# First token half of a decoder layer transposed straight from the loaded tiles, norm weights applied at the evacuation

## The chip, the cores and the metric

One NeuronCore of one Trainium2 chip runs the kernel. The metric is device time in microseconds; for the kernel before it is the median of three runs. All arithmetic is fp32. Every large product is done in three passes of fp32r matrix multiplications on a high and a low part of each operand (hi x lo, lo x hi, hi x hi), so each operand must be split in two before TensorE can use it.

## The reference, cut to what matters

```python
def rmsnorm(x, g):
    y = x * lax.rsqrt(jnp.mean(x * x, axis=-1, keepdims=True) + EPS)
    return y * g

n = rmsnorm(h, ln1_g)               # h: 1024 tokens x 1024 features
proj = n @ w_in                     # 1024 x 1536: pool | lru | gate columns
xc = causal_depthwise_conv(u_lru, conv_w, conv_b)
# y_pool from windowed means of u_pool; y_lru = rg_lru(xc, ...) * gelu(u_gate)
# rg_lru: r, i = sigmoid(xc @ w_a + b_a), sigmoid(xc @ w_i + b_i), then a linear scan over the tokens
h = h + concat(rmsnorm(y_pool), rmsnorm(y_lru)) @ w_out
h = h + (silu(n2 @ w_gate) * (n2 @ w_up)) @ w_down     # n2 = rmsnorm(h, ln2_g)
out = rmsnorm(h, lnf_g)
```

## The kernel before, in words

Tokens are in eight tiles of 128 (TT = 8), features in eight blocks of 128 (KT = 8). The input projection wants the normed input transposed, features on the partitions: `nT_hi` and `nT_lo`, 128 x 8 x 1024. It is made from units (c, i): column block c of `w_in` (twelve, of 128 columns; the lru columns first, then pool, then gate) by token half i (tiles 0 to 3, or 4 to 7). A unit is eight k-steps of three multiplications with 512 columns (`project`, L1622, through `three_pass`, L1598, lines 1602 to 1604). The order of the first units is (0,0), (1,0), (0,1), (1,1), then (2,0), (2,1) and so on (`UNITS`, L421).

Tile t of x is loaded whole by SP (L447 to L459), with the first two weight blocks between. Tiles 0 to 3 are only multiplied by the row of norm weights `g_row` (VectorE, `normalise`, L1124), since the root of the mean square of a token can be multiplied in later. Tiles 4 to 7 are multiplied by both (L1126), after ScalarE has squared and summed them (`x_squares`, L676, L669) and VectorE has made the reciprocal root (`variance`, `norm_rsqrt`). Each tile is transposed by TensorE in two lots of four 128 x 128 blocks, a bank each (`transposes`, L1609, L1619). ScalarE evacuates a bank as the high part (`nT_hi_part`, L662) and VectorE takes the difference as the low part (`nT_lo_part`, L1133). Weight blocks are split the same way: high part on ScalarE (`split_w`, L653), low part on GpSimd (L589).

The roots of tiles 0 to 3 are put on a diagonal (VectorE, L1167) and spread over the partitions by one product (`broadcast_roots`, L1698, L1700), which stands behind k-step 3 of unit (0,1). ScalarE copies it to `rb` (L703). `first_half` (VectorE, L1141) multiplies each unit of token half 0 by `rb` as it leaves its bank. On ScalarE the copy of `rb` stands in the queue ahead of the evacuations of units (0,0), (1,0) and (0,1), and of the split of weight block 2.

From the evacuated units of block j VectorE makes the convolution (`convolve`, L1199) and TensorE the gate products (`gates`, L1638, L1650): per call two fp32 multiplications, which show as four rows. `gates(j, 0)` waits for the convolution. Gates (0,0) stand behind unit (1,1) and ahead of unit (2,0); gates (0,1) behind unit (2,0). ScalarE takes the sigmoids (L751) and powers, VectorE the recurrence and its scan.

All queues are in order and written out by hand; semaphores tie them together. Then come the output projection, the FFN by Strassen-like products (L1730 to L1732) and the final norm; the change touches nothing of their order.

## Time and profile before

| | us |
|---|---|
| median of 3 runs | 925.41 |
| lowest, highest | 923.7, 925.44 |
| the profiled execution | 925.6 |
| its span, first to last instruction | 923.8 |
| TensorE busy in the span | 898.2 (97%) |
| VectorE, ScalarE, GpSimd busy | 617.0, 388.5, 317.3 |

Matrix multiplications are pipelined, so the rows of neighbours overlap: what one costs is the distance of its start from the next one's. Idle time is given with the instruction that ended it.

### The profile page before, as it was taken

To read this page: it belongs to the slowest core of one execution; us is meant where nothing else is said; L and a number is where in the kernel's file an instruction comes from. 1 tells how busy PE (TensorE), PEld (TensorE's weight loads), DVE (VectorE), ACT (ScalarE), POOL (GpSimd) and SP (SyncE) were. 2 spreads that over 40 slices of the span, in tenths; PEclk is the share of its full clock that TensorE was granted. 3 is DMA by queue.
4 is the path that set the end of the run, shared out by engine and by line. 5 is a ranking of instruction groups with operands and counts; after the bars stand their busy time and mean duration, and the time that the engine had idled before them with its cause. 6 is when DMAs were issued, how large, how long until landed. Compare 5 with 4: busy or idle time off the path is not lost.

```text
span 923.8 us, 10968 instructions
## 1 busy us (share of the span) xinstructions
PE 898.2 (97%) x3955; PEld 732.8 (79%) x3955; DVE 617.0 (67%) x822; ACT 388.5 (42%) x645; POOL 317.3 (34%) x227
## 2 busy tenths in 40 slices
PE   5989999999999999999999999999999999999996
PEld 4766777888888788888888888888888888888885
DVE  5568887546478865655665656656566986687766
ACT  5657623443365533323332323332334444444455
POOL 3023424364143655546555454545551000000000
PEclk9999999999999999999999999999999999999999
DMA  9011110203202132233322323224238943333324
GB/s 319 1 46 34 34 46 23 76 17 122 61 1 70 45 126 80 92 126 92 126 79 92 130 88 126 86 85 137 81 126 295 405 154 97 97 97 98 93 89 183
DMA packets 93790, 96.43 MB, mean 104 GB/s; under 512 B 5628, under 2 KB 63528, under 8 KB 93736
## 3 DMA queue, kind: packets, MB, share of 16 engines
q1 hardware_dynamic: 83224, 76.32, 24.3%
q10 hardware_dynamic: 10512, 19.40, 6.8%
q8 instruction: 32, 0.52, 0.2%
q14 instruction: 22, 0.18, 0.1%
HBM read 71.33 MB, written 24.38 MB: 104 GB/s over the span
## 4 chain that ended last, share of the span: by engine, by line
PE 91%; DVE 4%; issue 2%; ACT 1%; DMA 1%; POOL 0%; DVEq 0%; ACTq 0%
PE bank L1730 23%; PE bank L1731 23%; PE bank L1732 23%; PE bank L1602 7%; PE bank L1604 6%; PE bank L1603 6%; DVE xc L1199 2%; PE bank L1619 1%; PE bank L1650 1%; PE bank L1661 1%; DVE nT_lo L1133 1%; DMA g_row<-in_ln_g 1%; DVE xc L1124 0%; PE bank L1668 0%; ACT xc L734 0%
## 5 line engine op out<-in xcount | busy, mean ns | idle before, releaser
L624 POOL TENSOR_TENSOR r_lo<-wsum_S,r_hi 128x512 fp32r<-128x512 f32 x63 | 98.8, 1568 | 125.7 <-ACT r_hi L868 125.7
L624 POOL TENSOR_TENSOR r_lo<-gu_raw,r_hi 128x512 fp32r<-128x512 f32 x84 | 116.4, 1385 | 68.0 <-ACT r_hi L868 67.9
L1730 PE MATMUL bank<-T_hi,r_lo 128*128 128x512 f32 x336 | 130.9, 390 | 0.9 <-DVE u L1457 0.9
L1732 PE MATMUL bank<-T_hi,r_hi 128*128 128x512 f32 x336 | 130.7, 389 | 0.0
L1731 PE MATMUL bank<-T_lo,r_hi 128*128 128x512 f32 x336 | 130.7, 389 | 0.0
L1730 PE MATMUL bank<-d_hi,h_lo 128*128 128x512 f32 x308 | 119.8, 389 | 0.0
L1731 PE MATMUL bank<-d_lo,h_hi 128*128 128x512 f32 x308 | 119.8, 389 | 0.0
L1732 PE MATMUL bank<-d_hi,h_hi 128*128 128x512 f32 x308 | 119.8, 389 | 0.0
L868 ACT CAST r_hi<-gu_raw 128x512 fp32r<-128x512 f32 x84 | 52.3, 622 | 131.4 <-PE bank L1732 131.4
L1730 PE MATMUL bank<-nT_hi,r_lo 128*128 128x512 f32 x252 | 98.1, 389 | 0.0
L1731 PE MATMUL bank<-nT_lo,r_hi 128*128 128x512 f32 x252 | 98.0, 389 | 0.0
L1732 PE MATMUL bank<-nT_hi,r_hi 128*128 128x512 f32 x252 | 98.0, 389 | 0.0
L981 ACT CAST h_hi<-h_raw 128x512 fp32r<-128x512 f32 x76 | 47.2, 622 | 102.4 <-PE bank L1732 102.0
L1602 PE MATMUL bank<-nT_hi,w_lo 128*128 128x512 f32 x192 | 82.1, 428 | 2.4 <-DVE nT_lo L1133 2.4
L1435 DVE TENSOR_TENSOR h_lo<-h_raw,h_hi 128x512 fp32r<-128x512 f32 x76 | 52.4, 691 | 47.8 <-ACT h_hi L981 47.8
L1603 PE MATMUL bank<-nT_lo,w_hi 128*128 128x512 f32 x192 | 75.8, 395 | 0.0
L1604 PE MATMUL bank<-nT_hi,w_hi 128*128 128x512 f32 x192 | 75.7, 394 | 0.0
L1730 PEld LDWEIGHTS bank<-T_hi,r_lo 128*128 128x128 f32 x336 | 63.1, 188 | 14.7 <-POOL r_lo L624 1.3
L1731 PEld LDWEIGHTS bank<-T_lo,r_hi 128*128 128x128 f32 x336 | 63.1, 188 | 13.1
L1732 PEld LDWEIGHTS bank<-T_hi,r_hi 128*128 128x128 f32 x336 | 63.1, 188 | 13.0
L1732 PEld LDWEIGHTS bank<-d_hi,h_hi 128*128 128x128 f32 x308 | 57.8, 188 | 12.1
L1730 PEld LDWEIGHTS bank<-d_hi,h_lo 128*128 128x128 f32 x308 | 57.8, 188 | 12.0
(207 smaller groups left out, 1680.8 us busy)
## 6 DMA issues: line engine op xcount, KB each, us to landing
h_raw<-hid_ops ACTq DMA_DIRECT2D x72, 256.0 KB, 2.6
gu_raw<-in_w_ffn_gate SPq DMA_DIRECT2D x22, 512.0 KB, 3.7
gu_raw<-in_w_ffn_up SPq DMA_DIRECT2D x22, 512.0 KB, 4.8
hid_ops<-hid SPq DMA_DIRECT2D x44, 256.0 KB, 2.3
dn<-in_w_ffn_down SPq DMA_DIRECT2D x44, 256.0 KB, 10.8
hid_ops<-hsum_S SPq DMA_DIRECT2D x33, 256.0 KB, 2.6
w_raw<-in_w_in SPq DMA_DIRECT2D x12, 512.0 KB, 3.6
h<-in_x SPq DMA_DIRECT2D x8, 512.0 KB, 7.6
```

Source lines behind the costliest of these rows:

```text
L624: pool.tensor_tensor(lo_of(n)[:], a_block(f, name), f32(hi_of(n)[:]), ALU.subtract)\
L868: act.copy(hi_of(n)[:], a_block(f, name)).then_inc(r_hi_ok, 1)
L981: act.copy(h_hi[s % STEPS][:], h_source(s)[:]).then_inc(h_hi_ok, 1)
L1133: dve.tensor_tensor(nT_lo[dst], pt_of(n)[b][:].rearrange("p (k n) -> p k n", k=4), f32(nT_hi[dst]), ALU.subtract).then_inc(n_lo_ok, 1)
L1199: ins = dve.scalar_tensor_tensor(out=xc[j % 2][:], in0=ub[j % 2][:, off:off + S], scalar=v("conv_w", k * GT + j), in1=xc[j % 2][:], op0=AL ...
L1435: dve.tensor_tensor(h_lo[s % STEPS][:], h_source(s)[:], f32(h_hi[s % STEPS][:]), ALU.subtract)\
L1602: pe.matmul(bank, s_lo, m_hi, start=(k == 0), stop=False)
L1603: pe.matmul(bank, s_hi, m_lo, start=False, stop=False)
L1604: ins = pe.matmul(bank, s_hi, m_hi, start=False, stop=(k == n - 1))
L1730: pe.matmul(bank, s_lo, m_hi, start=(opens and j == 0), stop=False, skip_group_check=True)
L1731: pe.matmul(bank, s_hi, m_lo, start=False, stop=False, skip_group_check=True)
L1732: ins = pe.matmul(bank, s_hi, m_hi, start=False, stop=(closes and j == n - 1), skip_group_check=True)
```

## The change

Tiles 0 to 3 are loaded in left and right halves of 512 features. TensorE transposes each half as loaded, one bank of banks 2 to 5 for each tile, with no multiplication ahead of it. The norm weights are loaded as eight rows of 128, transposed on TensorE and copied to a column per feature block, `g_col`. The evacuation multiplies by them: four ScalarE operations of 128 columns with the column as scale in place of one cast of 512 (`first_hi`), and four VectorE operations in place of one (`first_lo`). The first two weight blocks are loaded and split in halves of four k-steps. Units (0,0) and (1,0) become four pieces of four k-steps (`project_first`): left halves of both units, then right halves; the right halves' transposes go between the k-steps of the first piece, those of tiles 4 and 5 into the third and fourth. The row of norm weights moves behind the fifth tile. The broadcast of the roots moves behind k-step 1 of unit (1,1). Gates (0,0) move behind unit (2,0). Two clears on GpSimd move behind the identity. In the FFN's down stage two semaphores of a pair of loads become one, with one threshold for both.

The diff, without the declarations of semaphores:

```diff
@@ -177,6 +177,8 @@
+g_rows = at("g_rows", 136.25, [KT, P])
+g_col = at("g_col", 140.25, [P, KT])
@@ -408,12 +419,19 @@
-FIRST_PT = ((6, 7), (0, 1), (2, 3), (4, 5))
 def pt_of(n):
-    return [psum[b] for b in (FIRST_PT[n] if n < 4 else (6, 7))]
+    return [psum[2 + n]] * 2 if n < 4 else [psum[6], psum[7]]
+def tile_count(n, b):
+    return 4 * b + n + 1 if n < 4 else 2 * n + b + 1
+def w_count(c):
+    return c + 3
 def sq_pos(n):
@@ -439,24 +457,26 @@
 def _(sp_q):
     def load_w_in(c):
-        if c >= 2:
-            sp_q.wait_ge(w_hi_ok, c - 1)
-            sp_q.wait_ge(w_lo_ok, c - 1)
+        sp_q.wait_ge(w_hi_ok, w_count(c - 2))
+        sp_q.wait_ge(w_lo_ok, w_count(c - 2))
...
-    def load_x(t):
+    def load_w_half(c, b, done_):
+        sp_q.dma_start(w_raw[:, c, KH * b:KH * (b + 1)], w_in_v[:, KH * b:KH * (b + 1), cols(COLS[c])])\
+            .then_inc(done_, 16)
+    for t in range(4):
+        sp_q.dma_start(h[:, t, 0:512], xf[cols(t), 0:512]).then_inc(x_left[t], 16)
+    for c in range(2):
+        load_w_half(c, 0, w_left[c])
+    for t in range(4):
+        sp_q.dma_start(h[:, t, 512:1024], xf[cols(t), 512:1024]).then_inc(x_in[t], 16)
+    for c in range(2):
+        load_w_half(c, 1, w_in_slot[c])
+    for t in range(4, TT):
+        if t == 5:
+            sp_q.dma_start(g_row[:], ln1_g.to_broadcast([P, D])).then_inc(grow_in, 16)
...
-    load_x(0)
-    load_x(1)
-    load_x(2)
-    load_w_in(0)
-    load_x(3)
-    load_x(4)
-    load_w_in(1)
-    load_x(5)
-    load_x(6)
-    load_x(7)
@@ -466,7 +486,7 @@
-    sp_q.wait_ge(zeroed, 2)
+    sp_q.wait_ge(zeroed, 3)
@@ -477,8 +497,8 @@
-            sp_q.wait_ge(w_hi_ok, NC_IN)
-            sp_q.wait_ge(w_lo_ok, NC_IN)
+            sp_q.wait_ge(w_hi_ok, w_count(NC_IN - 1))
+            sp_q.wait_ge(w_lo_ok, w_count(NC_IN - 1))
@@ -572,8 +592,6 @@
-    step(pool.memset(gate_w[0][:], 0.0))
-    step(pool.memset(gate_w[1][:], 0.0))
@@ -583,14 +601,22 @@
+    step(pool.memset(gate_w[0][:], 0.0))
+    step(pool.memset(gate_w[1][:], 0.0))
+    def split_w_half(c, b):
+        pool.wait_ge(w_hi_ok, 2 * b + c + 1)
+        k = slice(KH * b, KH * (b + 1))
+        pool.tensor_tensor(w_lo[c][:, k], w_raw[:, c, k], f32(w_hi[c][:, k]), ALU.subtract).then_inc(w_lo_ok, 1)
     def split_w(c):
-        pool.wait_ge(w_hi_ok, c + 1)
+        pool.wait_ge(w_hi_ok, w_count(c))
...
-    split_w(0)
-    split_w(1)
+    for b in range(2):
+        for c in range(2):
+            split_w_half(c, b)
@@ -652,6 +678,18 @@
+    def split_w_half(c, b):
+        act.wait_ge(w_in_slot[c] if b else w_left[c], 16)
+        k = slice(KH * b, KH * (b + 1))
+        act.copy(w_hi[c][:, k], w_raw[:, c, k]).then_inc(w_hi_ok, 1)
+    def first_hi(t, b):
+        act.wait_ge(xT_ok, tile_count(t, b))
+        for k in range(4):
+            ins = act.activation(nT_hi[:, 4 * b + k, cols(t)], pt_of(t)[b][:, cols(k)], ACT.Copy,
+                                 scale=g_col[:, 4 * b + k:4 * b + k + 1])
+        ins.then_inc(n_hi_ok, 1)
     def nT_hi_part(n):
@@ -674,18 +712,27 @@
     def x_squares(t):
+        if t < 4:
+            act.wait_ge(x_left[t], 16)
         act.wait_ge(x_in[t], 16)
         squares(t, t, sumA[:, PAD:])
-    act.dma_start(g_row[:], ln1_g.to_broadcast([P, D])).then_inc(grow_in, 16)
+    act.dma_start(g_rows[:], ln1_g.rearrange("o (k p) -> (o k) p", p=P)).then_inc(g_rows_in, 16)
+    act.wait_ge(consts, 2)
+    act.activation(early[:], ones[:], ACT.Sqrt)
+    act.wait_ge(gT_ok, 1)
+    act.copy(g_col[:], psum[1][:, 0:KT]).then_inc(g_col_ok, 1)
+    act.wait_ge(g_col_ok, 1)
+    for t in range(3):
+        first_hi(t, 0)
+    split_w_half(0, 0)
+    first_hi(3, 0)
+    split_w_half(1, 0)
+    for t in range(4):
+        first_hi(t, 1)
+    split_w_half(0, 1)
+    split_w_half(1, 1)
     act.wait_ge(consts, NCONST)
-    act.activation(early[:], ones[:], ACT.Sqrt)
-    nT_hi_part(0)
-    nT_hi_part(1)
-    split_w(0)
-    nT_hi_part(2)
-    nT_hi_part(3)
-    split_w(1)
     x_squares(4)
     x_squares(5)
     norm_sqrt(1, *BATCHES[0])
@@ -699,7 +746,7 @@
-    act.wait_ge(xs_ok, TT)
+    act.wait_ge(xs_ok, 4)
@@ -1112,19 +1159,15 @@
         rsqrt(var[:, lo:hi], sd[:, lo:hi], rstd[:, lo:hi], tmp[:, lo:hi], ready)
     def normalise(n, xs):
-        if n % TT >= 2:
+        if n % TT >= 2 and n not in (4, 5):
             dve.wait_ge(xT_ok, 2 * (n - 1))
-        if n == 0:
+        if n == 4:
             dve.wait_ge(grow_in, 16)
         if n == TT:
             dve.wait_ge(grow_in, 32)
             dve.wait_ge(proj_ok, 2 * NC_IN)
-        if n < 4:
-            dve.wait_ge(x_in[n], 16)
-            dve.tensor_tensor(xs[n % 2][:], h[:, n, :], g_row[:], ALU.mult).then_inc(xs_ok, 1)
-        else:
-            dve.scalar_tensor_tensor(out=xs[n % 2][:], in0=h[:, n % TT, :], scalar=rstd[:, n:n + 1],
-                                     in1=g_row[:], op0=ALU.mult, op1=ALU.mult).then_inc(xs_ok, 1)
+        dve.scalar_tensor_tensor(out=xs[n % 2][:], in0=h[:, n % TT, :], scalar=rstd[:, n:n + 1],
+                                 in1=g_row[:], op0=ALU.mult, op1=ALU.mult).then_inc(xs_ok, 1)
     def nT_lo_part(n):
         for b in range(2):
@@ -1140,15 +1183,20 @@
+    def first_lo(t, b):
+        dve.wait_ge(n_hi_ok, tile_count(t, b))
+        for k in range(4):
+            dst = (slice(None), 4 * b + k, cols(t))
+            ins = dve.scalar_tensor_tensor(out=nT_lo[dst], in0=pt_of(t)[b][:, cols(k)],
+                                           scalar=g_col[:, 4 * b + k:4 * b + k + 1], in1=f32(nT_hi[dst]),
+                                           op0=ALU.mult, op1=ALU.subtract)
+        ins.then_inc(n_lo_ok, 1)
+    dve.wait_ge(g_col_ok, 1)
+    for b in range(2):
+        for t in range(4):
+            first_lo(t, b)
...
-    normalise(0, xc)
-    normalise(1, xc)
-    normalise(2, xc)
-    nT_lo_part(0)
-    normalise(3, xc)
-    nT_lo_part(1)
-    nT_lo_part(2)
-    nT_lo_part(3)
@@ -1492,8 +1540,7 @@
     def down_sum(name, k):
...
-            dve.wait_ge(dn_in["22", k], 16)
-            dve.wait_ge(dn_in["12", k], 16)
+            dve.wait_ge(dn_in["22", k], 32)
@@ -1606,13 +1653,23 @@
+    def first_transposes(t, b):
+        if b == 0:
+            pe.wait_ge(x_left[t], 16)
+        else:
+            pe.wait_ge(x_in[t], 16)
+            pe.wait_ge(n_lo_ok, tile_count(t, 0))
+        for k in range(4):
+            ins = pe.transpose(pt_of(t)[b][:, cols(k)], h[:, t, cols(4 * b + k)], ident[:])
+        ins.then_inc(xT_ok, 1)
     def transposes(n, xs):
-        pe.wait_ge(xs_ok, n + 1)
+        pe.wait_ge(xs_ok, n - 3)
...
-            if 4 <= n <= TT:
-                pe.wait_ge(n_lo_ok, b + 1 if n == 4 else 2 * (n - 1) + b + 1)
+            if 5 <= n <= TT:
+                pe.wait_ge(n_lo_ok, 2 * (n - 1) + b + 1)
@@ -1622,7 +1679,7 @@
     def project(c, i, between=()):
...
-            pe.wait_ge(w_lo_ok, c + 1)
+            pe.wait_ge(w_lo_ok, w_count(c))
@@ -1686,24 +1743,44 @@
         three_pass(pj[n % 4][:], [(hi[:, k], lo[:, k], wo_hi[q][:, k], wo_low(q, k))
                                   for k in range(GT)]).then_inc(op_ok, 1)
-    pe.wait_ge(consts, NCONST)
+    def project_first(c, b, between=()):
+        pe.wait_ge(w_lo_ok, 2 * b + c + 1)
+        pe.wait_ge(n_lo_ok, 4 * (b + 1))
+        for k in range(KH * b, KH * (b + 1)):
+            n_hi, n_lo = nT_hi[:, k, half(0)], nT_lo[:, k, half(0)]
+            pe.matmul(pj[c][:], w_hi[c][:, k], n_lo, start=(k == 0), stop=False)
+            pe.matmul(pj[c][:], w_lo[c][:, k], n_hi, start=False, stop=False)
+            ins = pe.matmul(pj[c][:], w_hi[c][:, k], n_hi, start=False, stop=(k == KT - 1))
+            if k in between:
+                between[k]()
+        if b == 1:
+            ins.then_inc(proj_ok, 1)
+    pe.wait_ge(consts, 1)
+    pe.wait_ge(g_rows_in, 16)
+    pe.transpose(psum[1][:, 0:KT], g_rows[:], ident[0:KT, 0:KT]).then_inc(gT_ok, 1)
     for t in range(4):
-        transposes(t, xc)
-    project(0, 0, {6: lambda: transposes(4, xc)})
+        first_transposes(t, 0)
+    project_first(0, 0, {k: (lambda t=k: first_transposes(t, 1)) for k in range(4)})
+    pe.wait_ge(g_col_ok, 1)
+    project_first(1, 0)
+    project_first(0, 1, {5: lambda: transposes(4, xc)})
+    project_first(1, 1, {4: lambda: transposes(5, xc)})
     pe.wait_ge(rows_in, 16 * 8)
     pe.transpose(pg[0][:, 0:NROWS], vrows[0:NROWS, :], ident[0:NROWS, 0:NROWS]).then_inc(vT_ok, 1)
-    transposes(5, xc)
-    project(1, 0, {1: lambda: transposes(6, xc), 4: lambda: transposes(7, xc)})
+    transposes(6, xc)
+    transposes(7, xc)
     def broadcast_roots():
         pe.wait_ge(diag_ok, 4)
         pe.matmul(pg[1][:], ones_sq[:], diag[:], start=True, stop=True).then_inc(bcast_ok, 1)
-    project(0, 1, {3: broadcast_roots})
-    project(1, 1)
-    gates(0, 0)
+    project(0, 1)
+    project(1, 1, {1: broadcast_roots})
     for c in range(2, NC_IN):
         project(c, 0)
+        if c == 2:
+            gates(0, 0)
         if 0 <= c - 2 < GT:
             gates(c - 2, 1)
         if 0 <= c - POOL0 - 2 < GT:
```

## Rows read from the trace of the kernel before

**Rows 1.** The head of the page, and the chain that ended last, by engine

```profile
span 923.8 us, 10968 instructions
...
PE 91%; DVE 4%; issue 2%; ACT 1%; DMA 1%; POOL 0%; DVEq 0%; ACTq 0%
```

**Rows 2.** Busy time by stretch; after each engine's busy time the granted clock, DMA share, GB/s

```profile
17.00:20.50 3.50, 3.50 (x9) 2.73 (x10) 1.63 (x7) 3.08 (x8) 1.55 (x1) 0.51 1.15 321
27.50:31.00 3.50, 2.82 (x17) 2.10 (x16) 2.48 (x3) 2.44 (x6) 0.00 (x0) 1.00 0.00 0
51.00:54.50 3.50, 3.50 (x8) 1.83 (x7) 3.16 (x11) 1.65 (x3) 1.49 (x1) 0.52 0.21 56
120.00:200.00 80.00, 79.47 (x347) 63.41 (x346) 56.17 (x52) 27.75 (x38) 37.58 (x18) 1.00 0.15 47
```

**Rows 3.** TensorE in order of time: start, duration, line, operation, count

```profile
7.63 5.35 PE L1619 MATMUL bank<-ident,xc 128*128 128x128 f32 x24 [7.63 <-DVE xc L1124]
...
16.90 0.64 PE L1602 MATMUL bank<-nT_hi,w_lo 128*128 128x512 f32 x1 [2.41 <-DVE nT_lo L1133]
17.33 0.63 PE L1603 MATMUL bank<-nT_lo,w_hi 128*128 128x512 f32 x1
...
23.37 1.04 PE L1619 MATMUL bank<-ident,xc 128*128 128x128 f32 x8
...
26.55 1.16 PE L1619 MATMUL bank<-ident,xc 128*128 128x128 f32 x8 [1.26 <-DVE nT_lo L1133]
...
32.86 1.03 PE L1619 MATMUL bank<-ident,xc 128*128 128x128 f32 x8
...
38.51 1.02 PE L1700 MATMUL bank<-diag,ones_sq 128*128 128x512 f32 x2
...
39.61 0.40 PE L1603 MATMUL bank<-nT_lo,w_hi 128*128 128x512 f32 x1
...
47.35 0.39 PE L1604 MATMUL bank<-nT_hi,w_hi 128*128 128x512 f32 x1
50.34 2.99 PE L1650 MATMUL bank<-xc,gate_w 128*128 128x512 f32 x4 [2.60 <-DVE xc L1199]
...
60.61 0.79 PE L1602 MATMUL bank<-nT_hi,w_lo 128*128 128x512 f32 x1
```

**Rows 4.** DMA in the first 6 us

```profile
DMA packets 339, 1.26 MB, mean 210 GB/s; under 512 B 32, under 2 KB 32, under 8 KB 339
```

**Rows 5.** ScalarE in order of time

```profile
12.74 1.08 ACT L662 CAST nT_hi<-bank 128x512 fp32r<-128x512 f32 x2
...
15.05 1.06 ACT L653 CAST w_hi<-w_raw 128x1024 fp32r<-128x1024 f32 x1
15.99 1.07 ACT L669 ACTIVATE sumA<-h 128x1024 f32<-128x1024 f32 x1
...
39.57 0.59 ACT L703 COPY rb<-bank 128x512 f32<-128x512 f32 x1 [3.43 <-PE bank L1700]
...
72.04 0.69 ACT L751 ACTIVATE rg<-bank,vec 128x512 f32<-128x512 f32 x1
72.62 0.68 ACT L751 ACTIVATE ig<-bank,vec 128x512 f32<-128x512 f32 x1
```

**Rows 6.** VectorE in order of time

```profile
13.08 3.67 DVE L1133 TENSOR_TENSOR nT_lo<-bank,nT_hi 128x512 fp32r<-128x512 f32 x6
...
19.86 2.48 DVE L1126 SCALAR_TENSOR_TENSOR xc<-h,rstd,g_row 128x1024 f32<-128x1024 f32 x2
...
34.12 1.29 DVE L1133 TENSOR_TENSOR nT_lo<-bank,nT_hi 128x512 fp32r<-128x512 f32 x2 [1.76 <-ACT nT_hi L662]
...
37.11 0.88 DVE L1167 TENSOR_SCALAR diag<-ident,rstd 128x128 f32<-128x128 f32 x4
```

**Rows 7.** GpSimd in order of time, the third weight block

```profile
45.25 2.63 POOL L589 TENSOR_TENSOR w_lo<-w_raw,w_hi 128x1024 fp32r<-128x1024 f32 x1 [26.70 <-ACT w_hi L653]
```

More of the change, by code:

```diff
@@ L188, in sem @@
             return ctx.enter_context(nc.semaphore(name))
+        x_left = [sem(f"x_left{t}") for t in range(4)]
         x_in = [sem(f"x_in{t}") for t in range(TT)]
+        w_left = [sem(f"w_left{c}") for c in range(2)]
+        g_rows_in = sem("g_rows_in")
         rows_in, grow_in, small_in = sem("rows_in"), sem("grow_in"), sem("small_in")
@@ L198, in hymba_pool_rglru_block @@
         h_raw_in = [sem(f"h_raw_in{s}") for s in range(STEPS)]
-        dn_in = {bk: sem(f"dn_in{bk[0]}_{bk[1]}") for bk in DN_ORDER}
+        dn_in = {bk: sem(f"dn_in{bk[0]}_{bk[1]}") for bk in DN_ORDER if bk[0] != "12"}
+        for k in range(NP):
+            dn_in["12", k] = dn_in["22", k]
         stored = sem("stored")
@@ L215, in hymba_pool_rglru_block @@
         vec_ok = sem("vec_ok")
+        g_col_ok = sem("g_col_ok")
         u_ok = sem("u_ok")
@@ L266, in hymba_pool_rglru_block @@
         vT_ok = sem("vT_ok")
+        gT_ok = sem("gT_ok")
         bcast_ok = sem("bcast_ok")
@@ L986, in split_dn @@
                 if pr in ("M1", "M2", "M3"):
-                    act.wait_ge(dn_in[D_BLOCK[pr], k], 16)
+                    act.wait_ge(dn_in[D_BLOCK[pr], k], 32 if pr == "M3" else 16)
                 else:
```

## The prediction

> **What bounds the kernel now.** I read first the head of the page and its chain of waits [rows 1]: 91% of the chain that ended last is TensorE, in a span of 923.8 us; the profiled execution took 925.6 us, so 1.8 lie around the span, and the median of the runs shown is 925.41, 0.2 below it. The sum below is made against 925.6 and shifted by that 0.2. Next the stretches [rows 2]: between 120 and 200 us TensorE is busy 79.47 of 80 us. So a microsecond that TensorE gains or loses before about 120 us reaches the end, unless VectorE's chain of the mixer takes it back. Third, TensorE in order of time [rows 3]. The start holds four losses: nothing until 7.63; a stop from about 14.5 to 16.90; the half clock after it; and 2.60 us before the first gates at 50.34, again followed by a half clock. The granted clock is 0.51 and 0.52 in 17 to 20.5 and 51 to 54.5 and 1.00 in 27.5 to 31, where TensorE was busy 2.82 of 3.5 us [rows 2]: the 1.2 and the 2.4 GHz level. A product instruction takes 0.43 us at the lower one (16.90 to 17.33) and 0.228 at the higher: 34 steps from 39.61 to 47.35 [rows 3].
>
> **Step 1, the start.** Before, the 512 KB of the norm's row go first and the first multiplication waits for them. They leave the front; instead 4 KB of weights are loaded, transposed and copied to a column. By 6.0 us 1.26 MB had moved [rows 4]. The four left halves are 1.05 MB, so they are in by about 5.4 plus some 0.5 us, the first near 3.5 to 4. Identity and ones move ahead of two 0.5 us clears on GpSimd, hidden. I take ScalarE's first evacuation at 4.3.
>
> An evacuation of one bank was one cast of a 0.49 us pitch (two in 1.08) [rows 5]. It becomes four of 128 columns with a scale from the column. No such row exists. Bounds: a quarter of the cast each, 0.12, so 0.5 us a bank; from above the 0.69 of a sigmoid less 384 columns, 0.35 each, 1.4 a bank. The nearest row is the pair of sigmoids with one column operand, 72.04 to 72.62: 0.58 pitch at 512 columns; less the 384 columns that a piece lacks, at 0.88 ns each (a 1024-column cast has a pitch of 0.94, 15.05 to 15.99, so 512 columns cost 0.45), 0.24. That is 1.0 us a bank, and I take 1.05 with the last one's drain. VectorE: six banks in 3.67 us were 0.6 each; the four 128-column operations of the diagonal took 0.88 [rows 6], so 0.85 a bank (0.6 to 1.1).
> The Trainium skill, ScalarE: Activation LUTs, section What ACT_TABLE_LOAD costs, says that each pointer operand adds some 93 ns, whatever the columns; the rows agree (0.49 against 0.58). By its formula a bank would be 1.17 us and the sum some 0.3 us larger.
>
> So ScalarE: three banks 4.3 to 7.5, half a weight split 0.5, fourth bank to 9.1; VectorE to 10.2; GpSimd's half of a low part (half of the 2.63 of [rows 7]) is done by 9.6. The first product starts near 10.2, not 16.90: 6.7 us early.
>
> **Step 2, the right halves.** From 10.2 TensorE alternates three products and four transposes, at the lower clock at first: to 16.4 us. ScalarE's last bank follows to 17.6, two half splits to 18.6. Only then do the squares of x4 start: 18.6, before 15.99 [rows 5], **2.6 us later**. The lead of 6.7 is TensorE's only.
>
> **Step 3, the second token half.** Squares at 15.99 gave the first scaled tile at 19.86 + 1.24 = 21.1 [rows 6], 5.1 us later; it then waited for TensorE until 23.37 [rows 3]. After: 18.6 + 5.1 = 23.7, transposes at 23.9. TensorE has only two more k-steps by then, which themselves wait for GpSimd's low part of the right weight half (19.6), and from 21.0 it idles 2.9 us: the lead is gone. The chain of scale, transposes, cast and low part follows from 23.9. The transposes of tile 5 wait for tile 4's low part after the scaling of tile 6: about 28.6, before 26.55; tile 7's had waited 32.86 for products and come at 33.8. The second low part of tile 7 ends 3.0 later, near 36.8 (before 34.12 + 1.29 = 35.4). Products on the second half need all of them: 36.8 against 38.51 less twelve products of 0.228 = 35.8: **+1.0**.
>
> **Step 4, the clock.** Between 30 and 36.8 nothing but the transposes of tiles 6 and 7 is left for TensorE. I take the lower clock at 36.8: nine products at 0.43, not 0.228, **+1.8**. From below it is 0.
>
> **Step 5, the broadcast of the roots.** It stood behind four of eight k-steps of the first second-half unit; now it stands behind that unit and two k-steps: 30 products, not 12, 18 x 0.228 = **+4.1**. It comes at 38.51 + 1.0 + 1.8 + 4.1 = 45.4. The diagonal is ready at about 39 (before 37.11 + 0.88), so nothing asked for the delay.
>
> **Step 6, who is queued behind it.** ScalarE waits in order for the broadcast (39.57, after an idle 3.43) [rows 5]; behind it stand three evacuations and the split of the third weight block, whose low part on GpSimd ended at 45.25 + 2.63 = 47.88 [rows 7]. By +6.9 this is 54.8. Before, the gates at 50.34 hid it. Now the product behind which the gates are put needs it at once; TensorE is free at 36.8 + 48 x 0.228 + 1.8 + 0.9 (broadcast) = 50.4 and **idles 4.4 us**: one wait replaces the 2.6 of before. Then 24 products at first at the lower clock, 5.5 + 1.8 = 7.3, to 62.1. The gates' column input, ready at 50.3 before, is ready at 57.2: covered. Eight gate instructions at 0.43 (1.88 for four with the drain) are 3.4: the next unit starts at 65.5; before at 60.9 (60.61 in [rows 3] with the overlap of its start). **Sum +4.6**; VectorE's recurrence of head pair 0 moves by about the same, as it starts from those gates, so nothing gives it back.
>
> Other edits. More, smaller loads: SP issues all well ahead of their use; nothing. The norm's row lands near 14, first used past 22: nothing. The three small waits changed and the merged semaphores of the down stage: both blocks load in turn, and ScalarE's step there runs ahead: nothing, up to 0.3 us if it is late.
>
> Sum: 925.6 + 4.5 = 930.1 by the profiled execution, 929.9 by the median.
>
> **The rivals.** (a) The clock holds at 36.8, as it did with 2.82 of 3.5 us busy. Then the terms lose 1.8: +2.7 in the gates, and up to another 1.7 less where later TensorE stalls absorb it: 926.6 to 928.1, say 927.5. Against it: TensorE has under 2 us of work in the last 6. Chance 0.15.
> (b) Faster. The evacuation pieces cost near their lower bound, 0.5 us a bank, and the loads land early; ScalarE then has the squares at 14.6, 1.4 before their old time, and the second-half products start near 32.8, 3.0 early, with a warm clock. The broadcast is then only 1.1 late, and with 2.6 us saved before the gates the whole is 2 to 3 us shorter: 922.9. It decides from squares at about 15 us and the higher clock together. For it: TensorE's start is 6.7 us early for sure. Against it: the sigmoid row. Chance 0.14.
> (c) The two cancel, squares near 16 to 17: within 1.8 us, 925.4. Chance 0.13.
> (d) Pieces at their upper bounds, or low parts on VectorE held while GpSimd works: squares at 22, +7: 932.5. Chance 0.10.
> (e) The forecast, 0.48.
>
> **Numbers.** Measurements tell 0.2% (1.85 us) from no change. Faster: (b), 0.14. Same: (c) and a part 0.04 of (a), 0.17. Slower: the rest, 0.69. The range, from 924.0, which leaves out most of (b), to 932.0, which leaves out most of (d), holds about 0.8.
>
> **What would show it.** In the changed profile: first product near 10.2; squares of x4 near 18.6; TensorE idle some 3 us before tile 4's transposes; second-half products near 36.8 at a granted clock near 0.5; broadcast near 45; TensorE waiting 4 us on GpSimd's low part of the third block near 55. Wrong, if the squares start by 15 or the broadcast by 41: then the later stop is small and the gates' move wins.

## The result and the profile after

The changed kernel took 930.8 us (median of 4 runs, 930.02 to 931.72) against 924.74 us for the kernel before on the same chip: a ratio of 1.0063, 95% interval 1.0051 to 1.0075. It is slower, by 5.8 us by that ratio and 6.1 by the two medians. The forecast was 929.9 us, in a range of 924.0 to 932.0. The prediction started from a median of 925.41 for the kernel before, so what it forecast was a loss of 4.5 us. The profile is of the slowest of the four executions (931.72).

The head of the page, and the chain that ended last, by engine. They answer to [rows 1]:

```profile
span 929.9 us, 11022 instructions
...
PE 91%; ACT 3%; DVE 3%; issue 2%; POOL 1%; DMA 0%; ACTq 0%; DVEq 0%
```

The span is 6.1 us longer. The share of the chain says as little as it did before; the difference lies in the first 70 us. This is TensorE in order of time there, from its timeline (start, duration, line, operation, count, and the idle time before with what ended it). In the changed file L1663 is a transpose of a loaded half, L1751 a product of `project_first`, L1676 a transpose of tiles 4 to 7, L1649 a product of `project`, L1776 the broadcast, L1707 a gate product. The rows answer to [rows 3]:

```profile
7.59 1.11 PE L1663 MATMUL bank<-ident,h 128*128 128x128 f32 x4 [0.64 <-DMA h<-in_x]
11.29 0.77 PE L1751 MATMUL bank<-nT_lo,w_hi 128*128 128x512 f32 x1 [2.58 <-DVE nT_lo L1190]
...
26.02 1.09 PE L1676 MATMUL bank<-ident,xc 128*128 128x128 f32 x8 [2.61 <-DVE xc L1169]
...
30.60 1.10 PE L1676 MATMUL bank<-ident,xc 128*128 128x128 f32 x8
...
33.90 1.09 PE L1676 MATMUL bank<-ident,xc 128*128 128x128 f32 x8
36.05 1.16 PE L1676 MATMUL bank<-ident,xc 128*128 128x128 f32 x8 [1.06 <-DVE nT_lo L1176]
38.67 0.50 PE L1649 MATMUL bank<-nT_hi,w_lo 128*128 128x512 f32 x1 [1.47 <-DVE nT_lo L1176]
...
45.63 1.02 PE L1776 MATMUL bank<-diag,ones_sq 128*128 128x512 f32 x2
...
55.00 0.80 PE L1649 MATMUL bank<-nT_hi,w_lo 128*128 128x512 f32 x1 [4.22 <-POOL w_lo L614]
...
63.47 3.78 PE L1707 MATMUL bank<-xc,gate_w 128*128 128x512 f32 x8
66.69 0.79 PE L1649 MATMUL bank<-nT_hi,w_lo 128*128 128x512 f32 x1
```

Two rows of the kernel before that are compared here (the first product on the second token half, and the third stop for a convolution), and the third stop in the changed kernel:

```profile
35.79 0.39 PE L1602 MATMUL bank<-nT_hi,w_lo 128*128 128x512 f32 x1
98.12 1.98 PE L1650 MATMUL bank<-xc,gate_w 128*128 128x512 f32 x4 [1.20 <-DVE xc L1199]
```

```profile
104.21 1.98 PE L1707 MATMUL bank<-xc,gate_w 128*128 128x512 f32 x4 [1.18 <-DVE xc L1247]
```

What is to be seen. The first product starts at 11.29, not 16.90: 5.6 us early. Tile 4's transposes start at 26.02, not 23.37: the lead has become a lag of 2.7. The products on the second token half start at 38.67 against 35.8 before: +2.9. The broadcast comes 6.96 us behind them, before 2.7 us: +7.1 in all. Unit (2,0) starts at 55.00 after a stop of 4.22 us for a low part from GpSimd, and unit (2,1) starts at 66.69, before at 60.61: +6.1, which is the whole difference in span. Later the third stop for a convolution stands at 104.21 against 98.12, still +6.1, so nothing is given back.

ScalarE in order of time. L689 is the scaled evacuation, L684 the split of half a weight block, L707 the squares, L750 the copy of the roots, L679 the split of the third weight block. The rows answer to [rows 5]:

```profile
8.85 1.14 ACT L689 ACTIVATE nT_hi<-bank,g_col 128x128 fp32r<-128x128 f32 x4
9.86 0.63 ACT L684 CAST w_hi<-w_raw 128x512 fp32r<-128x512 f32 x1
13.80 1.14 ACT L689 ACTIVATE nT_hi<-bank,g_col 128x128 fp32r<-128x128 f32 x4 [3.31 <-PE bank L1663]
15.93 1.14 ACT L689 ACTIVATE nT_hi<-bank,g_col 128x128 fp32r<-128x128 f32 x4 [0.99 <-PE bank L1663]
17.55 2.27 ACT L689 ACTIVATE nT_hi<-bank,g_col 128x128 fp32r<-128x128 f32 x8 [0.48 <-PE bank L1663]
...
20.73 1.08 ACT L707 ACTIVATE sumA<-h 128x1024 f32<-128x1024 f32 x1
...
46.69 0.59 ACT L750 COPY rb<-bank 128x512 f32<-128x512 f32 x1 [7.28 <-PE bank L1776]
...
51.25 1.03 ACT L679 CAST w_hi<-w_raw 128x1024 fp32r<-128x1024 f32 x1
```

The squares of x4 start at 20.73, before at 15.99. ScalarE is idle 3.31, 0.99 and 0.48 us between the banks, since the evacuations in front of the squares wait for TensorE. In this trace the second-half products start 17.94 us behind these squares. Further on the copy of the roots follows an idle 7.28 us, and the split of the third block stands behind it until 51.25 (before 44.13).

GpSimd and VectorE around the third block, before in [rows 7]: L614 is the low part of a block, here two back to back, and L1247 the first convolution (from the two engines' timelines):

```profile
52.36 5.90 POOL L614 TENSOR_TENSOR w_lo<-w_raw,w_hi 128x1024 fp32r<-128x1024 f32 x2 [29.41 <-ACT w_hi L679]
```

```profile
51.46 7.88 DVE L1247 SCALAR_TENSOR_TENSOR xc<-ub,vec,xc 128x1024 f32<-128x1024 f32 x3 [2.80 <-ACT xc L781]
```

The first of the two low parts releases TensorE at 55.00. The convolution takes 7.88 us. In the kernel before it took 5.94, with one low part inside it:

```profile
44.34 5.94 DVE L1199 SCALAR_TENSOR_TENSOR xc<-ub,vec,xc 128x1024 f32<-128x1024 f32 x3 [2.80 <-ACT xc L734]
```

The granted clock by stretch (columns: stretch, its length, busy time of PE, PEld, DVE, ACT and POOL, granted clock, DMA share, GB/s), as [rows 2]:

```profile
11.20:16.80 5.60, 5.51 (x17) 4.53 (x18) 1.12 (x4) 2.01 (x8) 0.63 (x1) 1.00 1.06 412
26.00:30.40 4.40, 4.38 (x17) 3.46 (x17) 3.96 (x10) 2.21 (x5) 0.00 (x0) 0.62 0.21 63
31.00:38.60 7.60, 5.15 (x32) 3.83 (x30) 5.04 (x7) 6.14 (x11) 0.00 (x0) 1.00 0.01 2
38.60:50.60 12.00, 11.93 (x50) 9.31 (x50) 3.26 (x14) 4.45 (x11) 0.00 (x0) 1.00 0.00 0
55.00:61.30 6.30, 6.30 (x15) 4.95 (x16) 5.92 (x13) 0.68 (x1) 3.26 (x1) 0.51 0.56 166
```

After the 4.2 us stop TensorE runs at the lower level (0.51) for some 6.2 us, while the products from 38.6 ran at 1.00. The 1.00 of the first row can't be right: the products step by 0.43 us there (11.85, 12.28, 12.71), as they do from 55.00.

### The profile page after: what moved, and what is told of

It is laid out like the page before. It is cut to its first block, busy times and chain, and to the rows that moved or that the text cites. A ratio compares the mean times of both kernels' runs of the same rounds, so it can differ in the third digit from the quotient of the medians.

```text
span 929.9 us, 11022 instructions
## 1 busy us (share of the span) xinstructions
PE 902.5 (97%) x3956; PEld 734.4 (79%) x3956; DVE 615.3 (66%) x842; ACT 393.0 (42%) x672; POOL 318.2 (34%) x229
## 4 chain that ended last, share of the span: by engine, by line
PE 91%; ACT 3%; DVE 3%; issue 2%; POOL 1%; DMA 0%; ACTq 0%; DVEq 0%
PE bank L1807 23%; PE bank L1808 23%; PE bank L1809 23%; PE bank L1649 6%; PE bank L1651 6%; PE bank L1650 6%; PE bank L1676 1%; DVE xc L1247 1%; PE bank L1707 1%; PE bank L1718 1%; ACT nT_hi L689 1%; PE bank L1751 0%; PE bank L1725 0%; PE bank L1663 0%; ACT sumA L707 0%
## 5 line engine op out<-in xcount | busy, mean ns | idle before, releaser
L1649 PE MATMUL bank<-nT_hi,w_lo 128*128 128x512 f32 x176 | 75.1, 427 | 5.7 <-POOL w_lo L614 4.2
L1807 PEld LDWEIGHTS bank<-T_hi,r_lo 128*128 128x128 f32 x336 | 63.1, 188 | 14.7 <-POOL r_lo L650 1.3
L1650 PE MATMUL bank<-nT_lo,w_hi 128*128 128x512 f32 x176 | 69.7, 396 | 0.0
L1651 PE MATMUL bank<-nT_hi,w_hi 128*128 128x512 f32 x176 | 69.7, 396 | 0.0
## 6 DMA issues: line engine op xcount, KB each, us to landing
dn<-in_w_ffn_down SPq DMA_DIRECT2D x44, 256.0 KB, 10.2
```

The costliest lines, as they stand in the source:

```text
L1649: pe.matmul(bank, s_lo, m_hi, start=(k == 0), stop=False)
L1650: pe.matmul(bank, s_hi, m_lo, start=False, stop=False)
L1651: ins = pe.matmul(bank, s_hi, m_hi, start=False, stop=(k == n - 1))
L1807: pe.matmul(bank, s_lo, m_hi, start=(opens and j == 0), stop=False, skip_group_check=True)
```

## The experiments

All ratios are to the kernel before, run on the same chip in the same rounds. The median of the kernel before was 925.24 in the first group (e1 to e4), 925.57 in the second (e5 to e8) and 925.35 in the third.

The changed kernel was not run again in these rounds. Differences to it are differences of medians; by the ratios they come out up to 0.7 us otherwise (e1 6.0 instead of 5.7, e2 3.4 instead of 3.7, e7 4.3 instead of 3.6). The order of the kernels doesn't hang on that.

The start also varies from execution to execution. In e1, e2, e3 and e7 the code is the changed kernel's up to the second half, and in their traces the squares of x4 start at 19.96, 20.50, 19.84 and 20.32 and the second-half products at 37.91, 38.44, 37.78 and 38.25, against 20.73 and 38.67 in the changed kernel's trace.

**e1: the broadcast back.** In the changed kernel:

```diff
-            project(0, 1)
-            project(1, 1, {1: broadcast_roots})
+            project(0, 1, {3: broadcast_roots})
+            project(1, 1)
```

> The changed kernel with one thing undone: the broadcast of the roots stands again behind k-step 3 of unit (0,1). Theory A (the delay of the broadcast is passed on by ScalarE's queue to the third weight block, which unit (2,0) needs at once): the second-half products still start near 38.7 us, the broadcast comes at 41.4 instead of 45.63, the low part of the third block ends near 50.8 instead of 55.0, when TensorE comes free at 50.6; the wait of 4.2 us and the half clock behind it (2.9 us) both go, and the time falls by 6 to 7 us, to about 924. Theory B (the start decides: ScalarE's and VectorE's pieces make the second token half late): the broadcast only matters by its own 4.1 us or less, and the time stays near 927 to 930.

Measured: 925.11 us, ratio 0.9998 (0.9989 to 1.0007): 5.7 us below the changed kernel. TensorE's timeline:

```profile
37.91 0.50 PE L1649 MATMUL bank<-nT_hi,w_lo 128*128 128x512 f32 x1 [1.46 <-DVE nT_lo L1176]
...
40.76 1.02 PE L1776 MATMUL bank<-diag,ones_sq 128*128 128x512 f32 x2
...
50.19 0.50 PE L1649 MATMUL bank<-nT_hi,w_lo 128*128 128x512 f32 x1 [0.20 <-POOL w_lo L614]
...
55.77 3.78 PE L1707 MATMUL bank<-xc,gate_w 128*128 128x512 f32 x8
```

The broadcast follows 2.85 us behind the first second-half product, unit (2,0) starts at 50.19 after 0.20 us of waiting and at the full clock, and the gates come at 55.77 instead of 63.47. Taking the late broadcast back takes nearly the whole loss back, 5.7 us where 6 to 7 were expected. Theory A holds. The other two parts of the change nearly cancel, as e2 and e3 show.

**e2: the first gates back**, the broadcast left late:

```diff
+            gates(0, 0)
             for c in range(2, NC_IN):
                 project(c, 0)
-                if c == 2:
-                    gates(0, 0)
```

> The changed kernel with the first gates back ahead of unit (2,0), the broadcast left late. Theory A (the move of the gates helps, since it hides the convolution behind a unit): TensorE waits from 50.6 to 59.3 us for the convolution, and unit (2,1) starts 3.5 to 4 us later than in the changed kernel: about 934.5. Rival: the move of the gates costs (they come in a row with the next pair and wait for the sigmoids): the time falls or stays.

Measured: 934.51 us, ratio 1.0100 (1.0086 to 1.0114), 3.7 us above the changed kernel.

```profile
59.12 3.78 PE L1707 MATMUL bank<-xc,gate_w 128*128 128x512 f32 x4 [8.59 <-DVE xc L1247]
```

TensorE waits 8.59 us for the convolution here. The time is the expected one: the move of the gates helps, by hiding that wait behind a unit. Theory A holds.

**e3: both back**, so that only the new start is left:

> The changed kernel with the broadcast and the first gates both where they were: what is left is the new start alone. Theory A: the second-half products start near 38.7 us against 35.8 before, and all behind them keeps its distance: 2 to 3 us over the kernel before, 927 to 928. Rival (the new start is worth the 5.6 us by which the first product is earlier): 2 us or more under the kernel before.

Measured: 927.95 us, ratio 1.0031 (1.0019 to 1.0043). The second-half products start at 37.78 in its timeline, 2.0 us later than before, and the wait for the first convolution is the 2.60 of before. The new start loses 2.7 us by itself by the medians, and 2.2 between the profiled executions (927.79 and 925.6), although its first product is more than 5 us earlier. The rival, that the earlier first product would win, is refuted.

**e4: the kernel before with only the gates moved:**

> The kernel before with only the first gates moved behind unit (2,0). Theory A: unit (2,0) starts at 47.9 us, when its low part is ready, without a half clock; gates (0,0) and (0,1) follow at 53.4, and the next unit starts at 56.9 instead of 60.6: 3.5 to 4.5 us faster than the kernel before, about 921. Rival (VectorE's chain of the mixer sets the pace, so that TensorE's gain is taken back at the next gates): within 1 us of the kernel before.

Measured: 922.60 us, ratio 0.9971 (0.9961 to 0.9981): 2.6 us faster than the kernel before, and faster than the changed one by some 8. With e10 it is the fastest kernel of the study. The gain is less than the 3.5 to 4.5 expected. TensorE's timeline says where the rest went:

```profile
47.99 0.50 PE L1602 MATMUL bank<-nT_hi,w_lo 128*128 128x512 f32 x1 [0.20 <-POOL w_lo L589]
...
53.56 3.78 PE L1650 MATMUL bank<-xc,gate_w 128*128 128x512 f32 x8
56.78 0.79 PE L1602 MATMUL bank<-nT_hi,w_lo 128*128 128x512 f32 x1
...
78.46 1.98 PE L1650 MATMUL bank<-xc,gate_w 128*128 128x512 f32 x4 [1.19 <-DVE xc L1199]
...
95.14 1.98 PE L1650 MATMUL bank<-xc,gate_w 128*128 128x512 f32 x4 [1.19 <-DVE xc L1199]
```

Unit (2,1) starts at 56.78, 3.8 early. At the third set of gates TensorE waits 1.19 us instead of 0.37 and stands at 78.46 against 81.45, 3.0 early. VectorE's second convolution took 5.93 us, before 3.92; GpSimd's product with the input gate runs inside it from 58.15. Part of Theory A's gain is taken back by VectorE, as the rival said, but only 0.8 of 3.8. At 95.14 the kernel is still 3.0 ahead (98.12 before).

**e5: the squares early.** e1's kernel with ScalarE's and VectorE's work for x4 and x5 ahead of the last two right halves:

```diff
-            for t in range(4):
-                first_hi(t, 1)
-            split_w_half(0, 1)
-            split_w_half(1, 1)
             act.wait_ge(consts, NCONST)
+            first_hi(0, 1)
             x_squares(4)
+            first_hi(1, 1)
             x_squares(5)
             norm_sqrt(1, *BATCHES[0])
+            first_hi(2, 1)
+            first_hi(3, 1)
+            split_w_half(0, 1)
+            split_w_half(1, 1)
```

and on VectorE the variance and `norm_rsqrt(1)` in front of `first_lo(2, 1)`.

> The kernel of e1 (broadcast back, gates moved) with ScalarE's squares of x4 and x5 and their root put between the right halves' evacuations, in idle time of ScalarE, and VectorE's reciprocal root with them. Theory A (the squares, which queue behind all of tiles 0 to 3 on ScalarE, set the second token half): the first scaled tile is ready 1.5 to 2.5 us earlier, the second-half products start near 36.3, and the time falls by 1.5 to 2 us below e1's 925.1, to about 923.3. Rival (the chain of scale, transposes, cast and low part sets it, whenever the squares come, or the late low parts of the right halves do): within 0.7 us of e1.

Measured: 925.50 us, ratio 0.9998 (0.9990 to 1.0007): as e1 in time, a miss for Theory A. Timelines of TensorE, then VectorE and GpSimd:

```profile
23.93 1.04 PE L1681 MATMUL bank<-ident,xc 128*128 128x128 f32 x8
...
29.04 1.62 PE L1681 MATMUL bank<-ident,xc 128*128 128x128 f32 x8 [2.00 <-DVE nT_lo L1178]
...
33.97 1.09 PE L1681 MATMUL bank<-ident,xc 128*128 128x128 f32 x8
36.12 1.16 PE L1681 MATMUL bank<-ident,xc 128*128 128x128 f32 x8 [1.06 <-DVE nT_lo L1178]
38.75 0.49 PE L1654 MATMUL bank<-nT_hi,w_lo 128*128 128x512 f32 x1 [1.47 <-DVE nT_lo L1178]
```

```profile
21.65 4.02 DVE L1171 SCALAR_TENSOR_TENSOR xc<-h,rstd,g_row 128x1024 f32<-128x1024 f32 x2
```

```profile
21.08 3.50 POOL L610 TENSOR_TENSOR w_lo<-w_raw,w_hi 128x512 fp32r<-128x512 f32 x2 [9.47 <-ACT w_hi L684]
```

The squares started at 14.66 and tile 4's transposes at 23.93, 1.3 earlier than in e1, but by 33.97 the lead was gone. The two scalings took 4.02 us instead of 2.48, since they met GpSimd's low parts of the right weight halves (21.08 to 24.58); tile 5's transposes came at 29.04; TensorE, after 2.0 us of idle, ran the six products behind them at a step of 0.43, and tile 6's transposes stand behind those. So the squares' start was one of several things in a row. That the squares alone set the second token half is refuted for this start: they came 5.3 us earlier than in e1 and the second-half products 0.8 later. Which of the low parts, VectorE's chain and TensorE's order holds the rest is not shown.

**e6: whole banks.** The changed kernel with one cast and one subtraction per bank in `first_hi` and `first_lo`. The norm weights of tokens 0 to 511 are left out.

> The changed kernel with one cast and one subtraction of 512 columns per bank instead of four scaled pieces each; the norm weights of tokens 0 to 511 are left out. It measures what the pieces cost. Theory A: the first product comes 1.1 us earlier (11.29 to 10.2), the squares of x4 1.6 us earlier (20.73 to 19.1), all behind moves with them: about 929.2 against 930.8. Rival (TensorE's alternation of products and transposes at the half clock paces the right halves, the pieces hide in it): under 0.7 us.

Measured: 929.10 us, ratio 1.0045 (1.0032 to 1.0057), 1.7 below the changed kernel. The first product starts at 10.44, the squares at 18.52 and the second-half products at 36.44, each earlier than in the changed kernel's trace, the last two by 2.2. Theory A holds: the pieces cost about 1.7 us. In the changed kernel four of them take 1.14 us on ScalarE (row at 8.85) and 1.12 us on VectorE. In e6 the first product no longer waits for VectorE but for GpSimd's low part, 1.68 us.

**e7: the third block's split ahead of the wait**, the broadcast still late:

```diff
+            split_w(2)
             act.wait_ge(bcast_ok, 1)
...
                 evacuate(c, i)
-            split_w(2)
```

> The changed kernel, broadcast still late, but with ScalarE's split of the third weight block put ahead of its wait for the broadcast. Theory A (the late broadcast costs through ScalarE's queue: the split stands behind it and unit (2,0) needs its low part): unit (2,0) starts at 50.6 instead of 55.0, without a wait and without a half clock; the gates then wait for the convolution until about 59.2, so the next unit starts near 63 instead of 66.7: 3 to 4 us faster than the changed kernel, about 927.3. Rival (the convolution, late by as much, is the real bound): unchanged within 1 us.

Measured: 927.15 us, ratio 1.0017 (1.0008 to 1.0026), 3.6 below the changed kernel.

```profile
45.19 1.02 PE L1776 MATMUL bank<-diag,ones_sq 128*128 128x512 f32 x2
...
57.02 3.89 PE L1707 MATMUL bank<-xc,gate_w 128*128 128x512 f32 x8 [1.25 <-DVE xc L1247]
```

With the broadcast as late as ever, moving one cast in ScalarE's queue takes 3.6 us off, as Theory A said. The 4.2 us stop is gone; what remains is a wait of 1.25 for the convolution at 57.02. So 3.6 of the 5.7 us went through ScalarE's order, and that much is shown.

The way was not quite the expected one. GpSimd's low part of the third block now runs at 45.21, ahead of the first convolution, so that only one low part lies in it and it takes 5.95 us, not 7.88. The gates come at 57.02, not 59.2, and unit (2,1) starts at 60.34, 6.4 ahead of the changed kernel. Of that 1.7 is given back by the third stop for a convolution (99.58 against 104.21): on the way TensorE waits 0.59 us at 74.25 and 1.17 at 82.89, where the changed kernel's trace has one wait of 0.41 (87.53). No run takes apart the 2.0 us that are left between e7 and e1.

**e8: the kernel before with only the broadcast late:**

> The kernel before with only the broadcast of the roots moved behind k-step 1 of unit (1,1). Theory A: it comes 4.1 us later, the convolution and the gates behind it 4.1 later, and the longer idle stretch makes more of the next unit run at the half clock: 4 to 5.5 us slower than the kernel before, 929.5 to 930.7. Rival (the broadcast has slack ahead of the gates): under 2 us slower.

Measured: 932.48 us, ratio 1.0078 (1.0065 to 1.0090): 6.9 slower, more than expected. TensorE, VectorE and GpSimd:

```profile
42.61 1.02 PE L1700 MATMUL bank<-diag,ones_sq 128*128 128x512 f32 x2
...
56.35 3.78 PE L1650 MATMUL bank<-xc,gate_w 128*128 128x512 f32 x4 [8.59 <-DVE xc L1199]
```

```profile
48.44 7.85 DVE L1199 SCALAR_TENSOR_TENSOR xc<-ub,vec,xc 128x1024 f32<-128x1024 f32 x3 [2.80 <-ACT xc L734]
```

```profile
49.34 5.87 POOL L589 TENSOR_TENSOR w_lo<-w_raw,w_hi 128x1024 fp32r<-128x1024 f32 x2 [30.98 <-ACT w_hi L653]
```

The broadcast is 4.1 later, but the gates are 6.0 later, with a wait of 8.59 instead of 2.60. The first convolution took 7.85 us instead of 5.94. Late as it is, both low parts of GpSimd (5.87 us back to back) lie in it instead of one. e9 tests whether that is the cause.

**e9: the fourth block's split late.** e8's kernel with two lines of ScalarE's queue swapped, `sigmoids(0, 0)` ahead of `split_w(3)`:

> The kernel of e8 (kernel before, broadcast late) with ScalarE's split of the fourth weight block behind the first sigmoids, so that GpSimd's low part of it no longer runs inside VectorE's first convolution. Theory C (each GpSimd product or subtraction of 1024 columns inside a convolution lengthens it by 2 us; in e8 and in the changed kernel two lie in the first one, 7.9 us instead of 5.9): the first convolution takes 5.9 us, the gates come 1.9 us earlier, at 54.4, and the time is 2 us below e8's 932.5, less up to 2 us if the fourth block's low part now falls into the second convolution and that one is on the path. Rival (the length of the convolution has another cause, as the loads of that stretch): the first convolution stays at 7.9 us.

Measured: 930.04 us, ratio 1.0056 (1.0044 to 1.0069), 2.4 below e8 by the medians and 2.0 by the ratios. VectorE:

```profile
49.48 5.89 DVE L1199 SCALAR_TENSOR_TENSOR xc<-ub,vec,xc 128x1024 f32<-128x1024 f32 x3 [2.80 <-ACT xc L734]
...
58.61 5.93 DVE L1199 SCALAR_TENSOR_TENSOR xc<-ub,vec,xc 128x1024 f32<-128x1024 f32 x3
```

TensorE's wait in front of the gates fell from 8.59 to 6.63 us. They start at 55.42 and not at the 54.4 expected, since in this execution the broadcast itself came 1.0 later than in e8's (43.65). With one low part inside it the first convolution is back at 5.89; the second now meets the other and takes 5.93 instead of 3.92, which gives little back: the 2 us of the first one arrive in the time. Theory C holds.

**e10: the softplus ahead of the first convolution**, on top of e4:

```diff
-                    convolve(c)
                     if c == 0:
                         softplus()
+                    convolve(c)
```

> The kernel of e4 (kernel before, first gates behind unit (2,0)) with VectorE's softplus of the decay ahead of the first convolution, in its idle 2.8 us, instead of between the first and the second. Theory C: the second convolution starts 4 to 5 us earlier and ends before GpSimd's product with the input gate, so it takes 3.9 us, or 5.9 with the fourth block's low part inside, and the wait of 1.2 us for the third convolution near 78 shrinks: 0.5 to 1.5 us below e4's 922.6. Rival (the mixer's chain through the scans sets these waits): as e4, or up to 0.7 us slower, since the first convolution starts later.

Measured: 922.54 us, ratio 0.9974 (0.9965 to 0.9984): as e4. The wait for the third convolution did fall, from 1.19 to 0.41, but GpSimd's low part of the third block, now started beside the convolution, took 3.37 us instead of 2.63, and unit (2,0) waited 0.9 us for it, 0.7 more than in e4. The gain at one end was paid at the other, and the 0.5 to 1.5 us expected did not come.

The parts, in us:

| | late broadcast | broadcast as before |
|---|---|---|
| new start, gates moved | 930.8 (changed kernel) | 925.1 (e1) |
| new start, gates as before | 934.5 (e2) | 928.0 (e3) |
| old start, gates moved | not run | 922.6 (e4) |
| old start, gates as before | 932.5 (e8) | 925.2 (before) |

From the kernel before to the changed one by way of e3 and e1: the new start costs 2.7, the move of the gates gives 2.8 back, the late broadcast costs 5.7. The late broadcast costs 5.7 to 6.9 us in each pair that was run, and the move of the gates gives 2.6 to 3.7.

## Why the prediction was right

It named the way and the mechanism: the late broadcast holds up ScalarE's queue, the third block's low part comes late, and unit (2,0) waits for it. e1 and e7 show this. The places fit too: broadcast 45.4 and 45.63; unit (2,0) 54.8 and 55.00; the stop 4.4 and 4.22. The size fits less well than 929.9 against 930.8 suggests: +4.5 was forecast and +6.1 measured (5.8 by the ratio), and the median of the kernel before was 0.7 lower in the result than in the forecast. That the places fit to 0.2 us is in part luck, since two errors of 1.9 and 1.8 us, in steps 3 and 4, had opposite signs.

Two slips in the sums are small. Step 6 ends at +4.6 and the sum takes 4.5. And step 6 sets 65.5 against 60.9, where the row of the kernel before is 60.61: from start to start it forecast +4.9.

**Step 1.** The first product was put at 10.2 and came at 11.29. Most of that, 0.7, is that ScalarE's first evacuation started at 4.98 and not at 4.3; its transposes began at 3.76. A bank of pieces was put at 1.05 us on ScalarE and took 1.14 with its drain (three banks 4.98 to 8.32, so 1.11 each), so the sigmoid row with one column operand was the right neighbour, and the extra per operand that the Trainium skill states (ScalarE: Activation LUTs, What ACT_TABLE_LOAD costs) agrees with it: its formula gave 1.17. On VectorE it was put at 0.85 and took 1.12; the diagonal's rows, which read no bank, were too far a neighbour. The last left half was transposed at 7.59, after 0.64 us of waiting for its load, but cost nothing: ScalarE went from its third bank through the split (8.32) to the fourth (8.85) without a stop.

**Step 2.** The squares were put at 18.6 and started at 20.73. Beside the 1.1 us of step 1, TensorE stayed at a product step of 0.43 until 16.6, 5.3 us after its start; I had counted less, the 3.6 of the kernel before. That length varies: in e1 and e3 it was 3.5 us, and the squares started at 19.96 and 19.84, so at least 1.2 us of the error is in every trace of this start, and the rest is of the execution.

**Step 3** was mis-sized in its result: +1.0 predicted, +2.9 in the profiled execution, +2.0 in e3's, +2.7 us in e3's time. Its own length was right: 18.2 us from the squares to the second-half products predicted, 17.9 measured in the changed kernel and in e1, e2, e3, e6 and e7. The error was handed on from steps 1 and 2, by squares at 20.73 in place of 18.6. One thing inside the step was missed: after the idle 2.61 us TensorE ran nine products at the lower level (0.43 us each from 26.87), and tile 5's transposes followed them at 30.60 without a wait. The forecast put the lower level not here but at 36.8. And e5 shows that the chain doesn't simply follow the squares: with squares at 14.66 it took 24.1 us.

**Step 4** was wrong: +1.8 for a lower clock at the start of the second half. The clock was 1.00 there, although TensorE was busy 5.15 of the 7.6 us before. I had taken the work left in that stretch as under 2 us of the last 6; but tile 5's transposes came at 30.6, and the nine products of unit (1,1) and the transposes of tile 6 came behind them, up to 35.0.

**Step 5** was right: 6.96 us behind the first product against 2.73 + 4.1 = 6.8.

**Step 6** was right in mechanism, and e7 shows it. Its clock term was too small: some 15 products at 0.43, worth 3.0 us (24 products took 63.47 - 55.00 = 8.47, at the full step 5.47), where I had nine, worth 1.8. That and step 3 more than made up for step 4. The convolution was put at 57.2 and ended at 59.3, for a reason I did not see in the trace of before: a second GpSimd subtraction fell into it. Unit (2,0) still hid it.

**Rivals.** (a) said that the clock would hold at the second half, and it did (1.00). Its time, 927.5, did not come, since the squares were 2.1 us later than in the forecast and the lower clock after the late stop longer. (b), the faster side, asked for squares at 15 and cheap pieces. e6 has one whole cast a bank, the price that (b) gave, and squares at 18.5, and is still 1.0045 of before; e5 has squares at 14.7 and gained nothing on e1 by them. (c) asked for squares near 16 to 17; they came at 20.73. (d) had the right suspicion that VectorE is held while GpSimd works, at the wrong place: not at the low parts of the banks, but at the convolution. In the changed kernel the squares stayed below its 22.

Open is how much of the new start's 2.7 us is VectorE's chain and how much TensorE's order behind tile 5; e5 moved both and separated neither. Old start, gates moved and a late broadcast was not run.

## What to carry to other kernels

Making an engine's first instruction earlier is worth nothing where the next stage hangs on another engine's queue: find which instruction the following stage waits for, and ask when that one is issued (here the squares of x4, behind all evacuations of x0 to x3). Then ask the same of the instructions behind it: e5 issued the squares 5.3 us earlier and gained nothing. When a small step is moved back, list everything that stands behind it in every in-order queue that waits for it; here a 1 us product held up a weight split that stands behind three evacuated units in ScalarE's queue, and putting that split alone ahead of the wait gave 3.6 of 5.7 us back. Time two moves of a change apart: the gates' move was worth 2.6 us by itself and was buried under the other two.

## What the runs showed of the hardware

VectorE and GpSimd hold each other up when VectorE reads two operands from SBUF. The two-operand convolution steps are 3.92 us for three when GpSimd is idle (before, at 55.69), 5.94 with one GpSimd subtraction inside (e3), 7.88 with two (changed kernel), and 5.89 again when one was moved out (e9). GpSimd's 1024-column subtraction in turn took 2.46 us beside VectorE's subtractions from a bank (at 12.93 in the kernel before), 2.63 inside a convolution (at 45.25) and 3.37 where it started 0.13 us behind one (e10). VectorE's subtractions with one operand in a bank ran at 0.61 us each in [rows 6], while GpSimd's ran from 12.93 to 15.39 and from 16.18 to 18.55. The Trainium skill (SBUF — State Buffer, Who interferes with whom) states it as a rule: a VectorE instruction with two SBUF inputs contends with a GpSimd instruction that reads SBUF, and one with at most one SBUF input, outside the modes that use both ports, does not. These rows agree.

Even a tiny VectorE instruction can be held. The first one of the softplus behind the convolution, four columns (L1179 before, L1227 in the changed file), took 2.31 us at 50.20 in the kernel before, where GpSimd's subtraction ran from 50.05 to 52.48. It took 0.16 us at 59.26 in the changed kernel, where GpSimd had ended at 58.26.

The lower clock lasted for different times: about 3.6 us from 16.90 and 4 from 50.34 in the kernel before, 5.3 from 11.29, 4.3 from 26.02 and 6.2 from 55.00 in the changed one. It differs between executions of the same code too: from the first product on, 3.5 us in e1 (11.48 to 15.03) and 5.2 in e7 (11.04 to 16.27). In e10, whose start is that of the kernel before, the products step by 0.23 us from 17.21 to 18.14 and by 0.43 from 18.53 to 20.24, so the clock also fell in the middle of a busy stretch. And the granted clock of the first stretch is not to be read: it says 1.00 from 11.2 to 16.8 us, while products step by 0.43 us there, as they do at 0.51 from 55.0; the step between instructions decides.
